# Gate, queries, keys, values, first merge, attention, its merge and the low-rank inputs of each layer in one stage

## The reference, cut to what matters

```
p = h @ w_in                      # columns: z, xbc, dt, r k v, low-rank w a g, q k, v, gate logits
y = ssd_scan(xbc, dt)             # mixer A
y = rmsnorm(y * silu(z)) * norm_w
acc = sigmoid(h @ G0) * (y @ B0)  # merge 0
na = softmax(q k^T / 8 + bias) v  # mixer C, 16 heads; latent queries see all 512 keys, context queries 256
acc += sigmoid(h @ G2) * (na @ B2)# merge 2
low = shift(h @ w_low)            # then tanh (decay half) and sigmoid (gate half), for mixer B
rw = rwkv7(h @ w_rkv, low)
acc += sigmoid(h @ G1) * (rw @ B1)# merge 1
```

## Time and profile before

| | us |
|---|---|
| median of 3 runs (4583.14 to 4585.04) | 4583.78 |
| the profiled execution | 4582.91 |
| its span | 4581.1 |
| TensorE busy (89% of the span) | 4060.3 |
| VectorE busy (30%) | 1385.3 |
| ScalarE busy (23%) | 1032.1 |
| GpSimd busy (10%) | 455.0 |
| mean granted TensorE clock | 0.938 |

### The profile page before, as it was taken

How to read it: one execution, slowest core, us unless ns; L and a number is a source line. 1 busy time by engine, 2 the same in 40 slices (tenths; PEclk the granted TensorE clock), 3 DMA queues, 4 the chain that set the end, 5 groups by cost and what they waited for, 6 DMA issues and landing times. The chain is left out here.

```text
span 4581.1 us, 96000 instructions
## 1 busy us (share of the span) xinstructions
PE 4060.3 (89%) x42596; PEld 2729.8 (60%) x42596; DVE 1385.3 (30%) x2784; ACT 1032.1 (23%) x1747; POOL 455.0 (10%) x360
## 2 busy tenths in 40 slices
PE   6988988979999998959999598889889999978996
PEld 2453435437888785457878245655668887865332
DVE  2471003215555552110000145202145555512111
ACT  2111004213344331010000122103134443311101
POOL 0040011001111110000000002002011111100000
PEclk8999999989999998979999798899989999988998
DMA  7201222120100001348998630232110100036997
GB/s 293 73 1 56 73 64 61 42 93 20 32 20 19 18 3 57 125 151 300 318 316 282 257 115 32 83 110 61 50 48 18 32 20 18 3 106 261 398 403 274
DMA packets 299410, 539.10 MB, mean 118 GB/s; under 512 B 52320, under 2 KB 160112, under 8 KB 298880
## 3 DMA queue, kind: packets, MB, share of 16 engines
q1 hardware_dynamic: 291392, 505.80, 31.8%
q0 software_dynamic: 7616, 27.27, 1.6%
HBM read 515.13 MB, written 17.87 MB: 116 GB/s over the span
## 5 line engine op out<-in xcount | busy, mean ns | idle before, releaser
L1546 PE MATMUL bank<-inv 64*64 64x64 f32 x15104 | 488.3, 219 | 17.3 <-ACT inv L1834 8.5
L1546 PEld LDWEIGHTS bank<-inv 64*64 64x64 f32 x15104 | 467.6, 135 | 55.0 <-issue 52.7
L2688 PEld LDWEIGHTS bank<-xs,gu 128*128 128x128 f32 x3072 | 347.2, 193 | 8.6 <-issue 7.4
L2688 PE MATMUL bank<-xs,gu 128*128 128x96 f32 x3072 | 347.2, 276 | 1.0 <-DVE hid L2617 1.0
L1556 PE MATMUL bank<-sb_h,w 128*128 128x512 f32 (+1 forms) x768 | 321.1, 574 | 27.9 <-DMA w<-w_in 25.9
L263 PE MATMUL bank<-sb_h,ring 128*128 128x512 f32 (+1 forms) x768 | 313.7, 570 | 28.2 <-SPq L227 18.1
L263 PEld LDWEIGHTS bank<-sb_h,ring 128*128 128x128 f32 x768 | 149.2, 196 | 190.4 <-issue 176.1
L1556 PEld LDWEIGHTS bank<-sb_h,w 128*128 128x128 f32 x768 | 150.3, 197 | 184.6 <-issue 151.1
L552 PE MATMUL bank<-sb_h,ring 128*128 128x512 f32 (+1 forms) x512 | 178.9, 504 | 26.2 <-ACTq L564 20.8
L506 PE MATMUL bank<-sb_h,ring 128*128 128x512 f32 (+1 forms) x512 | 196.1, 544 | 5.4 <-SPq L227 3.6
L1299 DVE CUSTOM_DVE_ANT_0 sc<-bank,nabias 128x512 f32<-128x512 f32 (+1 forms) x96 | 53.9, 600 | 449.1 <-PE bank L1218 445.1
(11 more groups left out here) (389 smaller groups left out, 6125.0 us busy)
## 6 DMA issues: line engine op xcount, KB each, us to landing
mod_ring<-w_mod SPq DMA_DIRECT2D x24, 2048.0 KB, 22.4
ring<-w_in SPq DMA_DIRECT2D x24, 2048.0 KB, 7.8
gu<-moe_w_gate SPq DMA_DIRECT2D x128, 384.0 KB, 8.6
gu<-moe_w_up SPq DMA_DIRECT2D x128, 384.0 KB, 10.1
down<-moe_w_down SPq DMA_DIRECT2D x96, 512.0 KB, 4.5
gu<-moe_w_gate SPq DMA_DIRECT2D x64, 768.0 KB, 14.3
gu<-moe_w_up SPq DMA_DIRECT2D x64, 768.0 KB, 15.0
down<-moe_w_down SPq DMA_DIRECT2D x48, 1024.0 KB, 16.3
```

What stands on the lines that cost most here:

```text
L1546: m = mm(bank[hs, at:at + w], left(hs), right(hs), start=start, stop=True, skip_group_check=True)
L2688: m = mm(wide[j // 4][:, C * (j % 4):C * (j % 4) + C], w[:, P * j:P * j + P], xs[:, kt], start=kt == 0 and j % 4 == 0, stop=kt == KT - 1, ...
```

## The change

A new function `branch_streams` replaces gate, norm, merge 0, query, key and value projections, attention, merge 2 and the low-rank inputs. It is one stage with 43 semaphores and one stream of slabs on SyncE. TensorE's order is: gate, queries and keys with the sum of squares behind the second query tile, values, merge 0, attention, merge 2 with the two low-rank tiles ahead of its last output tile. In both merges the gate tiles run two ahead: G0 G1 P0 G2 P1 G3 P2 and so on (G gate, P output). The scores of the first attention unit come ahead of the last output tile of merge 0, and the first gate tile of merge 2 comes ahead of the last turn of attention. The bias buffer is zeroed at the stage's begin, and its first 16 transfers are issued between the requests for the keys' last and the values' first slab. The zeroing of the experts' rows in memory (layer 0, GpSimd) moves from the low-rank stage to the end of attention.

Besides, for every stage of the program: `phase` no longer ends with the barrier, and its semaphores are released one stage later; places in the ring are freed by the tile count itself; the loops of the convolution's projection, the output projection and the merges are written out. In the scan two scratch buffers now lie inside another one, and `low` is allocated before the ring.

```diff
 def phase(nc, names):
 
     _phase[0] += 1
-    with ExitStack() as st:
-        sems = namedtuple("Semaphores", names)(*(st.enter_context(nc.semaphore(f"{n}_{_phase[0]}")) for n in names.split()))
-        yield sems
-        for s in sems:
-            nc.sync.sem_clear(s)
-        nc.all_engine_barrier()
+    sems = namedtuple("Semaphores", names)(*(nc.alloc_semaphore(name=f"{n}_{_phase[0]}") for n in names.split()))
+    yield sems
+    for s in sems:
+        nc.sync.sem_clear(s)
+    for s in _cleared:
+        nc.release_semaphore(s)
+    _cleared[:] = sems
...
-            pe.wait_ge(s.tile_done, it * 8 + (4 * h + 4))
-            pe.sem_inc(free[h], 1)
+    for n in range(2, 2 * turns):
+        sp.wait_ge(s.tile_done, 4 * (n - 1))
+        sp.dma_start(k.ring[:, n % 2], wv[:, :, col0 + 512 * n:col0 + 512 * n + 512]).then_inc(loaded[n % 2], 16)
+    ask_next_slabs(k, sp, [(s.tile_done, 8 * turns - 4), (s.tile_done, 8 * turns)])
...
+def multiply_slabs(pe, nc, s, ring, rhs, banks, turns, emptied):
+
+    loaded = (s.loaded0, s.loaded1)
+    for n in range(8 * turns):
+        h, j = n // 4 % 2, n % 4
+        if j == 0:
+            pe.wait_ge(loaded[h], 16 * (n // 8) + 16)
+        if n >= 4:
+            pe.wait_ge(emptied, n - 3)
+        for kt in range(KT):
+            mm = nc.tensor.matmul(banks[j], ring[:, h, kt, P * j:P * j + P], rhs[:, kt], start=kt == 0, stop=kt == KT - 1)
+        mm.then_inc(s.tile_done, 1)
...
+def branch_streams(k, low, t0):
...
+        def _(sp):
+            def ask(place, at):
+                sp.dma_start(k.ring[:, place], w[:, :, at:at + 512]).then_inc(loaded[place], 16)
+
+            def ask_merge(b, m):
+                at = 256 * m
+                sp.dma_start(merge_slab(k, m % 2)[:, 0], w[:, :, C_GATE + D * b + at:C_GATE + D * b + at + 256]).then_inc(loaded[m % 2], 16)
+                sp.dma_start(merge_slab(k, m % 2)[:, 1], wb[:, b, :, at:at + 256]).then_inc(loaded[m % 2], 16)
...
+            take_first_slabs(k, sp, loaded, 16)
+            for h in range(2):
+                sp.wait_ge(s.z_done, 4 * h + 4)
+                ask(h, C_Q + 512 * h)
+            for h in range(2):
+                sp.wait_ge(s.qk_done, 4 * h + 4)
+                ask(h, C_Q + 1024 + 512 * h)
+            sp.wait_ge(s.cleared, 1)
+            ask_bias(0)
+            ask_bias(1)
+            for h in range(2):
+                sp.wait_ge(s.qk_done, 4 * h + 12)
+                ask(h, C_V + 512 * h)
+            for m in range(4):
+                sp.wait_ge(*((s.v_done, 4 * m + 4) if m < 2 else (s.proj_done, 2 * m - 2)))
+                ask_merge(0, m)
+            for m in range(2):
+                sp.wait_ge(s.proj_done, 2 * m + 6)
+                ask_merge(2, m)
+            for f in range(2, KT):
+                sp.wait_ge(s.scored, 2 * last_unit[f - 2] + 2)
+                ask_bias(f)
+            for m in range(2, 4):
+                sp.wait_ge(s.proj2_done, 2 * m - 2)
+                ask_merge(2, m)
+            sp.wait_ge(s.proj2_done, 6)
+            sp.dma_start(k.ring[:, 0, :, 0:2 * P], w[:, :, C_WA:C_WA + 2 * P]).then_inc(s.loaded0, 16)
...
             nc.gpsimd.memset(bias[:], 0.0).then_inc(s.cleared, 1)
+            for f in range(KT):
+                pool.wait_ge((s.bias0, s.bias1)[f % 2], 128 * (f // 2 + 1))
+                dst = bias[:, f % 2, :, LC:]
                 nc.gpsimd.tensor_tensor(dst, dst, mask, ALU.add).then_inc(s.added, 1)
                 pool.wait_ge(s.added, f + 1)
                 nc.gpsimd.tensor_scalar(dst, dst, 8.0, None, ALU.mult).then_inc(s.masked, 1)
+            if l == 0:
+                pool.wait_ge(s.weighed, 2 * NU)
+                nc.gpsimd.memset(blank, 0.0).then_inc(s.zero, 1)
+                pool.wait_ge(s.zero, 1)
+                for i in range(EXPERTS * SLOTS // P):
+                    nc.gpsimd.dma_start(k.d.rows_in[P * i:P * i + P], blank).then_inc(k.pool_dma.zeroed, 16)
+                pool.wait_ge(k.pool_dma.zeroed, 16 * (EXPERTS * SLOTS // P))
...
+            def tile(out, left, right, done):
+                for kt in range(KT):
+                    mm = nc.tensor.matmul(out, left(kt), right(kt), start=kt == 0, stop=kt == KT - 1)
+                mm.then_inc(done, 1)
+
+            def slab(h, j):
+                return lambda kt: k.ring[:, h, kt, P * j:P * j + P]
+
+            def gate_z():
+                for j in range(8):
+                    if j % 4 == 0:
+                        pe.wait_ge(loaded[j // 4], 16)
+                    if j >= 4:
+                        pe.wait_ge(s.silu_done, j - 3)
+                    tile(k.bank[j % 4][:, t0:], slab(j // 4, j % 4), lambda kt: k.h[:, kt, t0:], s.z_done)
+
+            def queries_and_keys():
+                for j in range(16):
+                    h, a = j // 4 % 2, first[j // 8]
+                    if j % 4 == 0:
+                        pe.wait_ge(loaded[h], 16 * (j // 8) + 32)
+                    pe.wait_ge(*((s.silu_done, j + 5) if j < 4 else (s.qk_out, j - 3)))
+                    tile(k.bank[j % 4][:, a:], slab(h, j % 4), lambda kt: k.h[:, kt, a:], s.qk_done)
+                    if j == 1:
+                        pe.wait_ge(s.summed, KT - 1)
+                        nc.tensor.matmul(sums, const(k, "ones"), ssq[:, t0:], start=True, stop=True).then_inc(s.sum, 1)
+
+            def values():
+                for j in range(8):
+                    h, t = j // 4, j % 4
+                    if t == 0:
+                        pe.wait_ge(loaded[h], 64)
+                    pe.wait_ge(*((s.qk_out, j + 13) if j < 4 else (s.root, 1)))
+                    tile(k.bank[j], lambda kt: k.h[:, kt, P * t:P * t + P], lambda kt: k.ring[:, h, kt], s.v_done)
+
+            def gate(b, t):
+                h, j = t // 2 % 2, t % 2
+                if j == 0:
+                    pe.wait_ge(loaded[h], 32 * (t // 4) + 96 + 32 * b)
+                if t >= 2:
+                    pe.wait_ge(sig_done[b], t - 1)
+                tile(gates[b][j][:, 0:n], lambda kt: merge_slab(k, h)[:, 0, kt, P * j:P * j + P], lambda kt: k.h[:, kt, t0:], gate_done[b])
+
+            def proj(b, t):
+                h, j = t // 2 % 2, t % 2
+                if t >= 2:
+                    pe.wait_ge(merged[b], t - 1)
+                tile(projs[b][j][:, 0:n], lambda kt: merge_slab(k, h)[:, 1, kt, P * j:P * j + P], lambda kt: y[:, kt, t0:], proj_done[b])
+
...
-                if h == 0 and u >= 2:
-                    pe.wait_ge(s.yturned, u - 1)
+                if h == 0:
+                    pe.wait_ge(*((s.yturned, u - 1) if u >= 2 else (s.merged, KT)))
...
-            scores(0)
+            gate_z()
+            queries_and_keys()
+            values()
+            pe.wait_ge(s.v_out, 8)
+            gate(0, 0)
+            gate(0, 1)
+            pe.wait_ge(s.scaled, KT)
+            for t in range(KT):
+                if t == KT - 1:
+                    scores(0)
+                proj(0, t)
+                if t + 2 < KT:
+                    gate(0, t + 2)
+            pe.wait_ge(s.sig_done, KT)
...
-            if NU >= 2:
-                pe.wait_ge(s.yturned, NU - 1)
+            pe.wait_ge(s.scored, 2 * NU)
+            gate(2, 0)
+            pe.wait_ge(s.yturned, NU - 1)
             turn_y(NU)
+            gate(2, 1)
+            pe.wait_ge(s.yturned, NU)
+            for t in range(KT):
+                proj(2, t)
+                if t + 2 < KT:
+                    gate(2, t + 2)
+                if t == KT - 2:
+                    pe.wait_ge(s.loaded0, 208)
+                    for j in range(2):
+                        tile(T[j], slab(0, j), lambda kt: k.h[:, kt], s.low_done)
...
+            def gate_z():
+                for j in range(KT):
+                    act.wait_ge(s.z_done, j + 1)
+                    if j >= 2:
+                        act.wait_ge(s.multiplied, j - 1)
+                    ac(zs[:, j % 2, t0:], k.bank[j % 4][:, t0:], ACT.Silu).then_inc(s.silu_done, 1)
+                    if j:
+                        square(j - 1)
+                square(KT - 1)
+
+            def queries_and_keys():
+                for j in range(16):
+                    act.wait_ge(s.qk_done, j + 1)
+                    ac(qk[:, j, first[j // 8]:], k.bank[j % 4][:, first[j // 8]:], ACT.Copy).then_inc(s.qk_out, 1)
+                    if j == 1:
+                        act.wait_ge(s.sum, 1)
+                        inverse_root(k, act, rinv[:, t0:], sums, s.root)
...
+            def sigmoid(b, t):
+                act.wait_ge(gate_done[b], t + 1)
+                if t >= 2:
+                    act.wait_ge(merged[b], t - 1)
+                ac(sg[:, t % 2, t0:], gates[b][t % 2][:, 0:n], ACT.Sigmoid).then_inc(sig_done[b], 1)
...
+            gate_z()
+            queries_and_keys()
+            values()
+            act.wait_ge(s.multiplied, KT)
+            for t in range(KT):
+                sigmoid(0, t)
             powers(0)
             powers(1)
```

(41 more changed lines are left out.)

479 lines of the change are left out of this document (135 added, 344 removed).

## The result

The changed kernel takes 4440.21 us (median of 4 runs, 4435.15 to 4443.11), the kernel before on the same chip 4584.38 (4 runs, 4583.14 to 4585.04): ratio 0.9685, 95% interval 0.9668 to 0.9701. 4456 was predicted, with 4443 as the low end. The gain is 144 us where 128 was forecast, and in three other sets of runs the unaltered changed kernel took 4437.73, 4437.05 and 4440.58. So it is no accident of one set that the forecast was some 17 us too high.

The account below looks back on a forecast made before the run. TensorE's order was taken as the path, with time lost at stage borders and in half-clock matmuls behind them. 112.0 us inside the stage plus 16.0 outside, 128.0, gave 4456 us (chance 0.50), range 4443 to 4474.

Parts of the forecast that it names:

- step 11: Outside the new stage: 8.5 us from unrolled loops and borders, 3.6 from barriers, 3.9 from clears, 16.0 in sum.
- step 3: Values straight behind the keys: 31.7 us of standing and 5.4 of slow tiles gone, 37.1 us over both layers.
- step 4: Start of the queries: 3.6 us of standing and 1.8 of slow first slab gone, 5.4 us.
- step 7: Low-rank inputs: weights asked for after output tile 5, so 15.3 us of standing goes and four tiles speed up, 20.5 us.
- Steps 1 and 2: Norm hidden beside the queries, 25.2 us; full clock for the first matmuls after norm and after attention, 7.4 us.
- Steps 4 to 6: Starts of queries (5.4 us) and attention (5.2 net, value-copy wait costing 2.0), and attention's end (5.7).
- Step 8: Slab borders inside the new stage: TensorE no longer waits for its own last matmul before freeing a slab, 11.1 us.
- Step 9: New stage's exit to the RWKV heads: 12.4 us against 12.8 idle, 0.8 gained over both layers, at 0.061 a clear.
- Step 10: Layer 1's merges: slabs 2 and 3 come too late, a new wait of 1.7 us each, costing 6.8 us.
- The rival that these waits drop the clock: The four late-slab waits in layer 1's merges are followed by half speed, 1.8 us each: 4463 us, chance 0.15.
- barriers worthless: Removing barriers gives nothing outside the stage and clears cost 0.1 us: 4467 us, chance 0.12.
- The rival of a held-down clock: Without pauses TensorE's granted clock is held down in the new stage; 4604 us at 20% half speed; slower, chance 0.03.

## Why the prediction was wrong, and where it was right

The step that failed is step 11, "Outside it": 8.5 for loops and own waits, 3.6 for barriers, 3.9 for freed clears, "Sum 16.0". The two runs that put these back cost 14.4 and 13.2 us, 27.6 together (the second also includes the new stage's own ends, under 1 us by the prices), and the profiles of the pair give 31.4 outside the stage. The bounds given there, 0 and 7.5 for barriers and clears, left out the upper side, and the 8.5 had no upper bound at all.

Both parts of it were too small, the stops and the clock. Summed over the prediction, some 26 us of the 128.0 were slow matmuls made fast (7.4 of step 2, 5.4 of step 3, 1.8 of step 4, 5.2 of step 7, 0.8 of the sums, and 5.8 in the tiles at borders, 2.4 of these outside the stage), and 102 were stops. Outside the stage, then, some 13.6 us of stops and 2.4 of slow matmuls had been priced, and 18.6 and 12.7 came. (Modulation blurs this: it is busy 3.4 us less and stands 2.4 more, in the waits for its own transfers. Without it, 21.0 and 9.3 came.)

- The stops before the first matmul of the stages outside, the heads left out, are 11.3 us shorter in sum, where the 7.5 of barriers and clears stood for them. The largest single one is before the scan, 6.88 to 5.41 us in each layer; the old ends bring back 0.57 us of it and the old loops 0.67, and for the loops' part step 11 had no term.
- The slow matmuls were priced only in the tiles at slab borders. The runs show them behind stage starts as well: the output projection of layer 1 takes 27.89 us in the changed kernel, 29.48 with the old ends and 29.82 with the old loops.

Over the whole kernel the standing looks well forecast, 103.6 us less between the means of two profiles before and four after, where 102 had been said, while TensorE is busy 41.7 us less with the same 42596 matmuls, where 26 had been said. That agreement is luck: inside the stage the standing fell 85.2 us and not 88, outside it more than priced. What makes the matmuls behind a stop slow is not settled. Its length alone is not it: with every semaphore cleared twice TensorE stands longer before the output projection of layer 1 than with the old loops, and runs at full clock (27.89 us, granted clock 1.00) all the same.

```profile
4003.04 27.89 PE L266 MATMUL bank<-sb_acc,ringb 128*128 128x256 f32 x128 [2.13 <-SPq L231]
```

Nor is all of the excess pinned to a cause: 5.1 and 4.2 us of the two experiments lie in the scan and the heads, whose code is unchanged, and how much of that is chance stays open.

By step:

- Steps 1 and 2, norm and clock: right. The stops are gone, and exposing the norm costs 20 to 21 us, where 25.2 with the borders had been priced. The first tiles behind are at full clock.
- Step 3, values: right, 110.2 us and no stop, where 110.1 and none were said.
- Steps 4 to 6: right at their places (no stop at queries, scores or the last turn; 1.4 for the value copies, where 2.0 were said). But "Attention's inside, with its bias reloads, is unchanged" was wrong by some 3 us of standing (L1144 28.9 to 30.0 in four profiles, 26.4 and 26.2 before). In layer 1 the third bias is asked for at 3044.64, GpSimd can begin on it 9.5 us later and ends at 3059.35, where VectorE and behind it TensorE wait for it. Before the change the same took 7.1 us (3154.95 to 3162.05). Now a slab is asked for 2.4 us ahead of it, at 3042.24; that the two get in each other's way is likely, but no run separates them.
- Step 7, low-rank: right, no wait; taking it back costs 10.4 us in layer 0, 10 said.
- Step 8, borders inside: no stop is left.
- Step 9: 12.48 and 11.39 us before the heads, 12.4 said, so right in layer 0 and 1.0 too high in layer 1; doubling the clears gave 0.061 and 0.057 us for one, where 0.061 was said.
- Step 10: right in place and size, 7.0 against 6.8 us. The rival that these waits drop the clock holds for one in four, the longest. The estimate of 6.8 us for a slab, worked out from what the Trainium skill ("DMA: Bandwidth & Descriptors", anatomy of the GpSimd path) states for the other path of issue, and by which no wait would come, doesn't hold for these transfers of SyncE: with 6.9 us of cover TensorE waits 1.4 to 2.7 us.

Inside the stage the sum was 112.0 and 114.1 came; that it is so close is in part luck, since the standing fell by 3 us less than priced and the busy time by 5 more, and the two nearly cancel. The rival "barriers worthless" (4467) was wrong in direction: the ends gave more than priced and not less. The rival of a held-down clock is out: in the stage 0.99 was granted in layer 0 (0.96 before) and 0.96 to 0.97 in layer 1 (0.92).

## What to carry to other kernels

Price a stop twice: its idle time, and the matmuls behind it, which may be slowed by the clock even after a stop of 2 us (56.8 instead of 55.2 us here). A program of many short stages loses on the way into most of them. Before a long tail of semaphore clears, let the next stage's transfers be issued; and when tiles are reordered, count how many lie between the last use of a buffer and the next need of it, for the shortest tile size.

## What had not been expected of the hardware

- The same stop can be followed by either clock. Before the output projection of layer 0, TensorE stands 2.26 us in all four profiles of the changed kernel, and the projection then takes 56.81, 55.20, 56.84 and 56.78 us, at a granted clock of 0.97, 1.00, 0.97 and 0.97; behind 2.48 us, with the old stage ends, it took 55.20. In layer 1, behind 1.73 us, it takes 27.9 in all four, and behind 2.13 us, with doubled clears, as well; behind 1.91, 2.27 and 2.78 us in other kernels it was slow (15.77 for the first slab; 29.48 in all; 15.67 for the first slab).
- Chance of this kind moves unchanged stages by 2 to 5 us between executions (heads of layer 1, 725.5 and 721.8), while the whole spans of the two executions before lie 3.8 us apart and those of the four after up to 9.1.
- One semaphore clear takes SyncE 0.057 to 0.061 us, and one small strided transfer's issue 0.66 us (10.60 for 16).
